# A state space layer inside a two-block transformer kernel, computed in chunks of four steps

## The reference

```python
bu = einsum('blgh,gph->blgp', u, bbar)            # drives, complex: re and im
x[t] = a * x[t-1] + bu[t]                         # scan over 256 steps, complex
y = einsum('blgp,ghp->blgh', xr, c_re) - einsum('blgp,ghp->blgh', xi, c_im) + d * u
y = gelu(y);  z = y @ w_glu + b_glu
out = z[:, :512] * sigmoid(z[:, 512:])
```

## Time and profile before

| | |
|---|---|
| profiled execution, its own time | 882.28 us |
| span, first to last instruction | 880.5 us |
| mean granted PE clock | 0.962 |
| busy: PE / PEld / DVE / ACT / POOL | 826.3 / 710.2 / 574.8 / 396.5 / 299.3 us |
| matmuls, vector, scalar, POOL instructions | 4933 / 856 / 614 / 248 |

### The profile page before, as it was taken

One profiled execution on the slowest core, in us unless ns is written; L12 is line 12 of the kernel. 1 busy time (PEld: TensorE's weight loads), 2 busy tenths in 40 slices (PEclk: granted clock), 3 DMA queues, 4 the chain that ended last, 5 costly groups with the idle time before them and its releaser, 6 DMA issues.

```text
span 880.5 us, 12434 instructions
## 1 busy us (share of the span) xinstructions
PE 826.3 (94%) x4933; PEld 710.2 (81%) x4933; DVE 574.8 (65%) x856; ACT 396.5 (45%) x614; POOL 299.3 (34%) x248
## 2 busy tenths in 40 slices
PE   7999999999999989999989998769896999999996
PEld 6889988998788889877778896435585999999884
DVE  4755957565674589656565569997657666666552
ACT  5644346334554433433774451212356544444441
POOL 3042801899010199998000024665401011111010
PEclk9999999999999999999999999787698999999998
DMA  7897893487305545645454642000244555665541
GB/s 205 194 249 240 193 243 85 121 187 173 96 26 194 164 127 191 211 121 164 144 192 144 190 156 84 1 0 1 71 144 143 161 176 177 182 192 192 192 167 48
DMA packets 77820, 130.79 MB, mean 149 GB/s; under 512 B 4286, under 2 KB 28210, under 8 KB 77634
## 3 DMA queue, kind: packets, MB, share of 16 engines
q1 hardware_dynamic: 76418, 125.10, 49.4%
q0 software_dynamic: 1200, 4.83, 1.7%
q10 hardware_dynamic: 144, 0.07, 0.0%
HBM read 128.91 MB, written 1.06 MB: 148 GB/s over the span
## 4 chain that ended last, share of the span: by engine, by line
PE 83%; DVE 11%; issue 2%; ACT 1%; DMA 1%; POOL 1%; DVEq 0%; SPq 0%; POOLq 0%; ACTq 0%
PE ps L1327 41%; PE ps L1344 16%; PE ps L1359 14%; PE ps L1446 2%; PE ps L1429 2%; PE ps L1580 2%; DVE ssm_b L1107 1%; DVE w_lo L762 1%; DVE ssm_a L1104 1%; PE ps L1273 1%; PE ps L1457 1%; PE ps L1458 1%; PE ps L1459 1%; DVE ssm_a L1099 1%; DVE ssm_b L1100 1%
## 5 line engine op out<-in xcount | busy, mean ns | idle before, releaser
L762 DVE TENSOR_TENSOR w_lo<-stage,w_hi 128x1024 fp32r<-128x1024 f32 x232 | 301.8, 1319 | 192.2 <-ACT w_hi L524 191.7
L524 ACT ACTIVATE w_hi<-stage 128x1024 fp32r<-128x1024 f32 x232 | 243.4, 1060 | 264.1 <-PE ps L1327 117.2
L1327 PE MATMUL ps<-w_hi,act_t 128*128 128x512 f32 (+1 forms) x768 | 253.5, 393 | 3.7 <-DVE act_t L799 2.1
L1327 PEld LDWEIGHTS ps<-w_hi,act_t 128*128 128x128 f32 x768 | 145.2, 190 | 38.0 <-issue 4.8
L1327 PE MATMUL ps<-w_lo,act_t 128*128 128x512 f32 (+1 forms) x448 | 174.8, 390 | 0.0
L1344 PE MATMUL ps<-act_t,w_hi 128*128 128x256 f32 x832 | 151.9, 284 | 2.5 <-DVE w_lo L762 2.5
L1344 PEld LDWEIGHTS ps<-act_t,w_hi 128*128 128x128 f32 x832 | 130.9, 193 | 3.0 <-DVE w_lo L762 2.7
L1359 PE MATMUL ps<-act_t,w_hi 128*128 128x256 f32 x704 | 127.4, 284 | 0.0
L1344 PE MATMUL ps<-act_t,w_lo 128*128 128x256 f32 x416 | 117.6, 283 | 0.0
L1359 PEld LDWEIGHTS ps<-act_t,w_hi 128*128 128x128 f32 x704 | 110.1, 192 | 0.0
L1359 PE MATMUL ps<-act_t,w_lo 128*128 128x256 f32 x352 | 99.7, 283 | 0.0
(11 more groups left out here) (309 smaller groups left out, 1201.7 us busy)
## 6 DMA issues: line engine op xcount, KB each, us to landing
stage<-in_even_w_in SPq DMA_DIRECT2D x64, 512.0 KB, 5.8
stage<-in_odd_w_in SPq DMA_DIRECT2D x48, 512.0 KB, 4.3
stage<-in_w_gate_up SPq DMA_DIRECT2D x44, 512.0 KB, 4.5
stage<-in_w_down SPq DMA_DIRECT2D x22, 512.0 KB, 3.9
stage<-in_even_w_out SPq DMA_DIRECT2D x16, 512.0 KB, 3.8
stage<-in_odd_w_out SPq DMA_DIRECT2D x16, 512.0 KB, 3.7
stage<-in_w_in SPq DMA_DIRECT2D x10, 512.0 KB, 3.6
stage<-in_w_out SPq DMA_DIRECT2D x8, 512.0 KB, 4.4
```

The lines of the kernel that those rows point to most:

```text
L524: nc.scalar.activation(w_hi[:, u % RING, :], stage[:, u % RING, :], ACT.Copy).then_inc(hi_ready, 1)
L762: nc.vector.tensor_tensor(w_lo[:, u % RING, :], stage[:, u % RING, :], w_hi[:, u % RING, :].bitcast(F32), ALU.subtract).then_inc(lo_ready, 1)
L1327: ins = mm(out[:, b, :], left, right, start=(k == 0 and n == 0), stop=(k == k_tiles - 1 and n == 2))
```

## The change

The 256 tokens are cut into 64 chunks of four steps. The state is scanned over the 64 chunk ends alone; what happens inside a chunk is matmul work with constants.

- **Constants.** POOL multiplies B and C by powers of the decay `a`: three for B, four for C (`times_a`, six operations of 128x512 each). PE turns four instead of one B (`turn_b`: 16 transposes after the second half of the queries, 16 after the keys of the dilated attention), and ACT copies them, eight copies of 128x512. After the retention keys PE makes the lag matrices (what an input does to the next three outputs within a chunk): 64 matmuls into 32 rows each, 32 or 96 columns wide; ACT copies them, POOL adds the skip term and makes the last power of C. The waves are only 64 long: two calls of `waves` instead of eight, one set of three ACT operations instead of four.
- **Drives.** `ssm_drives`: 128 matmuls of 32 input rows and 64 columns, between the queries' and the keys' projection; four in turn use the four strips of 32 rows and write to four banks. DVE then does four rounds (`ssm_drive`, `ssm_scan`) instead of 16, with the same tile sizes as one step before.
- **Outputs.** `ssm_lags`: 16 matmuls of 128 input rows and 256, 192, 128 or 64 columns, ahead of the attention. `ssm_states`: four times 32 matmuls into 32 rows, 63 columns wide, three between the heads and one behind them. They add up in PSUM, where ACT reads them for the gelu; the skip operation on DVE is gone.
- **Order.** ACT and DVE split the weights of the second half of `mix_attn` ahead of the turned result of the state space layer.
- **End.** The last three units of the last chunk are multiplied for the first 128 tokens, then for the second; the squares, the root and the output of the first block follow on their own.

All four rounds of drives and the rotation of the keys now stand ahead of the first head, and only the last scan behind it. The core of the diff, first POOL and ACT, then PE, DVE and the end of PE's program:

```diff
+            def times_a(dst, src, tmp, conj):
...
+                for own, other, op in ((0, 1, ALU.add if conj else ALU.subtract), (1, 0, ALU.subtract if conj else ALU.add)):
+                    TT(part(tmp[:, 0, :]), part(src[:, own, :]), ar, ALU.mult)
+                    then(TT(part(tmp[:, 1, :]), part(src[:, other, :]), ai, ALU.mult))
+                    ins = TT(dst[:, own, :], tmp[:, 0, :], tmp[:, 1, :], op)
...
+            then(nc.gpsimd.memset(lag[:], 0.0))
+            pool.wait_ge(b_wide_ready, 2)
+            for k in (1, 2):
+                times_a(b_pow[k], b_pow[k - 1], pow_tmp_early, False).then_inc(b_pow_ready, 1)
+                pool.wait_ge(b_pow_ready, k)
             scale_gates(0)
...
-            for i in range(3):
-                waves(i)
+            times_a(b_pow[3], b_pow[2], b_turn[:, 3, :, :, :].rearrange("p c t n -> p c (t n)"), False).then_inc(b_pow_ready, 1)
...
+            pool.wait_ge(b_turned, 2)
+            for k in (2, 3):
+                times_a(c_pow[k], c_pow[k - 1], c_pow[4], True).then_inc(c_pow_ready, 1)
...
+                    for part in range(2):
+                        ahead((("qb", "kb")[part], 1))
+                        act.wait_ge(b_turned, part + 1)
...
+                        for i in range(4):
+                            nc.scalar.activation(b_turn[:, 2 * part + i // 2, i % 2], bank(4 + i).rearrange("p (t n) -> p t n", t=CT), ACT.Copy).then_inc(b_ready, 1)
...
+            for part, kind in enumerate(("qb", "kb")):
+                for c in range(2):
+                    channels((kind, c))
+                turn_b(part)
+            pe.wait_ge(b_ready, 8)
             values_and_attention(1)
...
+            def ssm_drives():
+
+                chunk_drained(pe, ("u", 0))
+                for ct in range(CT):
+                    for c in range(2):
+                        for j in range(STEP):
+                            for q in range(4):
+                                r = slice(32 * q, 32 * q + 32)
+                                ins = mm(drive[:, ct, c, q, :], b_turn[r, STEP - 1 - j, c, ct, :], u_p[r, ct, j, :], start=(j == 0), stop=(j == STEP - 1))
+                ins.then_inc(drive_done, 1)
+
+            def ssm_lags():
+
+                pe.wait_ge(drive_read, CT)
+                pe.wait_ge(lag_ready, 1)
+                for ct in range(CT):
+                    for k in range(STEP):
+                        mm(y_of(ct)[:, k:STEP, :], lag[:, k, ct, :], u_p[:, ct, 0:STEP - k, :], start=(k == 0 and ct % 2 == 0), stop=False, skip_group_check=True)
+
+            def ssm_states(ct):
+
+                pe.wait_ge(state_ready, ct + 1)
+                for j in range(STEP):
+                    for c in range(2):
+                        for q in range(4):
+                            r = slice(32 * q, 32 * q + 32)
+                            ins = mm(y_of(ct, r)[:, j, 1:NC], c_pow[j + 1][:, c, ct * P + 32 * q:ct * P + 32 * q + 32], ssm_a[:, ct, c, q, 0:NC - 1],
+                                     start=False, stop=(c == 1), skip_group_check=True)
...
+            def ssm_between(i, part):
+                if part == 1 and i in (1, 3, 5):
+                    ssm_states(i // 2)
...
+            for ct in range(CT):
+                ssm_drive(ct)
+                if ct < 2:
+                    ssm_scan(ct)
+            chunk_drained(dve, ("skv", 0))
+            rope(SINK_H, KV_H)
+            ssm_scan(2)
...
+            for b in range(NB):
+                tok = slice(b * P, (b + 1) * P)
+                for j in range(KF // 2 - DOWN_LAST, KF // 2):
...
+                ins.then_inc(block_done, 1)
```

More of the change, by code:

```diff
@@ L48 @@
 UNIT = 1024
-SSM_BUFS = 4
-SSM_EARLY = 6
-SSM_STEPS = (2, 2) + 9 * (1,)
+STEP = 4
+NC = S // STEP
 AHEAD = 3
+DOWN_LAST = 3
 MASKS_AT, TABLES_AT = 20, 42
@@ L465, in _ @@
             root(1, D)
-            for i in range(3, 8):
-                waves(i)
+            pool.wait_ge(lag_copied, 4)
+            skip = mixed[:, 1, 0:512].rearrange("p (t n) -> p t n", t=CT)
+            for ct in range(CT):
+                ins = nc.gpsimd.tensor_scalar(skip[:, ct, :], ident[:], col[:, COL_SKIP + ct:COL_SKIP + ct + 1], None, ALU.mult)
+            then(ins)
+            nc.gpsimd.tensor_tensor(lag[:, 0], lag[:, 0], skip, ALU.add).then_inc(lag_ready, 1)
+            pool.wait_ge(lag_ready, 1)
+            then(times_a(c_pow[4], c_pow[3], b_pow[0], True))
+            then(nc.gpsimd.tensor_tensor(sp["fade"][:], sp["mag"][:], sp["mag"][:], ALU.mult))
+            then(nc.gpsimd.tensor_tensor(sp["fade"][:], sp["fade"][:], sp["fade"][:], ALU.mult))
+            nc.gpsimd.memset(fade[:, :, 0:1], 0.0)
+            nc.gpsimd.tensor_scalar(fade[:, :, 1:NC], sp["fade"][:].unsqueeze(2).to_broadcast([P, ST, NC - 1]), 1.0, None, ALU.mult).then_inc(fade_ready, 1)
             for h in range(RET_H):
@@ L472, in _ @@
                 nc.gpsimd.tensor_tensor(ret_rstd[:, h, :], ret_rstd[:, h, :], neg_half[:, 0:2], ALU.pow).then_inc(ret_scale, 1)
+            pool.wait_ge(late_in, 16 * 3)
+            pool.wait_ge(ret_decayed, RET_H)
+            for i in range(2):
+                waves(i)
             root(2, D)
@@ L656, in _ @@
             split_hi(chunks[("u", 0)][0] + 5)
+            act.wait_ge(wave_ready, 1)
+            then(nc.scalar.activation(cos_t, sin_t, ACT.Abs))
+            nc.scalar.activation(sin_t, sin_t, ACT.Sin)
+            nc.scalar.activation(cos_t, cos_t, ACT.Sin, bias=half_pi[:], scale=-1.0).then_inc(wave_sin, 1)
             act.wait_ge(h_ready, 2)
@@ L712, in _ @@
             nc.scalar.activation(gate_z[:], gate_z[:], ACT.Sigmoid).then_inc(sig_ready, 1)
-            ahead(("glu", 0))
+            ahead(("mix_attn", 1))
             hi_of_turned(3 * KD + 20, 4, 4, COL_GSSM)
@@ L746, in _ @@
             ahead(("down", 1))
-            chunk_done(act, ("down", 1))
-            squares_half_down(1, 0, result(("down", 1))[:, 0, :]).then_inc(squared, 1)
-            act.wait_ge(down_scaled_b, 1)
-            squares_half_down(1, 1, result(("down", 1))[:, 1, :]).then_inc(squared, 1)
+            for b in range(NB):
+                act.wait_ge(block_done, b + 1)
+                squares_half_down(1, b, result(("down", 1))[:, b, :]).then_inc(block_squared, 1)
         @block.vector
@@ L1479, in _, with turn_b @@
             pe.wait_ge(c_ready, 1)
-            pe.wait_ge(b_ready, 1)
             values_and_attention(0)
-            for name in (("qb", 0), ("qb", 1), ("kb", 0), ("kb", 1)):
-                channels(name)
+            def turn_b(part):
+                pe.wait_ge(heads_out, 2)
+                pe.wait_ge(b_wide_ready, 2)
+                pe.wait_ge(b_pow_ready, 2 * part + 1)
+                if part:
+                    pe.wait_ge(b_ready, 4)
+                for i in range(4):
+                    for ct in range(CT):
+                        ins = nc.tensor.transpose(bank(4 + i, P, ct * P), b_pow[2 * part + i // 2][:, i % 2, ct * P:(ct + 1) * P], ident[:])
+                ins.then_inc(b_turned, 1)
+            for part, kind in enumerate(("qb", "kb")):
[3 more added lines that the diff above has]
+            pe.wait_ge(b_ready, 8)
             values_and_attention(1)
@@ L1653, in _ @@
                 start_chunk(name)
-                for j in range(KF // 2):
+                for j in range(KF // 2 - c * DOWN_LAST):
                     tokens_unit(name, j, lambda k: ff_hi[:, k, :], lambda k: ff_lo[:, k, :], KF, lambda k: pe.wait_ge(ff_lo_ready, k // 2 + 1))
+            for b in range(NB):
+                tok = slice(b * P, (b + 1) * P)
+                for j in range(KF // 2 - DOWN_LAST, KF // 2):
+                    hi, lo = unit_of(name, j)
+                    for i in range(2):
+                        k = 2 * j + i
+                        passes = ((ff_hi[:, k, tok], hi[:, i, :]), (ff_hi[:, k, tok], lo[:, i, :]), (ff_lo[:, k, tok], hi[:, i, :]))
+                        for n, (left, right) in enumerate(passes):
+                            ins = mm(result(name)[:, b, :], left, right, start=False, stop=(k == KF - 1 and n == 2))
+                ins.then_inc(block_done, 1)
 _INPUTS = [
```

288 lines of the change are left out of this document (144 added, 144 removed).

## The result

The changed kernel takes 834.72 us (median of 4 runs, 831.95 to 841.16); the kernel before took 881.27 (878.98 to 882.96) beside it, with a fourth execution added to the three known before. The ratio is 0.9482, with a 95% interval of 0.9446 to 0.9517.

A forecast was written before the change was run, and what follows sets the result against it. DVE was taken to set the pace of the state space and window attention stage, PE that of the rest. 882.28 + 9.1 - 32.8 - 2.1 = 856.5 us, so 855 at the median; eight-in-ten range 841 to 874.

The forecast's parts named there:

- the heads' pace: Window attention: two heads depend on the two before, 8.1 us per period, two periods.
- Behind the turned result nothing changes in size: After the state space result is turned: no time change; the gelu reads PSUM in place of SBUF.
- Up to the drives: PE's path before the mixing stage: 9.1 us more, from B's transposes 3.1, a wait 2.3, lag matrices 3.7.
- Both at nothing: POOL's early powers and the later powers that replace the waves: no cost to PE.
- Drives: Start of the mixing stage: 32 groups of four row strips at 0.23 us each, 7.4 us.
- the end: Behind the last matmul: one square and two additions remain, 2.1 us less.
- The prediction's other price for the drives: From the Trainium skill: about threefold for four row strips, making the drives about a third longer than 7.4 us.
- The rival of column strips one after another: Lag matrices and state blocks on PE: strips run singly, 36.2 us more, 891 us; chance 0.06.
- The stage goes back to full clock and groups cost their columns: Mixing stage on PE: full clock, small-matmul groups priced by columns, 839 us; chance 0.16.
- Two at a time: Small matmuls on PE run only in twos, group terms of 19.2 us double, 874 us; chance 0.11.
- the fourth rival: Heads keep waiting on DVE operations slowed by POOL, or the early wait costs over 2.3 us: 866 to 880; chance 0.07.
- the early wait: PE's wait for `b_ready` 8, ahead of `values_and_attention(1)`, for ACT's last four copies of B: 2.3 us.

The follow-up runs named there:

- The kernel before with shorter waves: Kernel before, with the waves' angle reduction on POOL left out, nothing else moved: 876.35 against 882.58 us, ratio 0.9949.
- keys first: Changed kernel with DVE rotating the keys behind two of four rounds and lag products behind the second pair's scores: 832.11 us, ratio 0.9442.
- blocks behind: Changed kernel with the first three state blocks behind the next pair's scores instead of ahead of them: 833.08 us, ratio 0.9448.
- fillers: Changed kernel with 70 unused matmuls of 128 columns put into PE's wait for the keys: 841.78 us, ratio 0.9543.
- half drives: Changed kernel with drives of 32 instead of 64 columns, the same in number: 838.36 us in one execution.
- the serial run: Changed kernel with drives, lag matrices and state blocks doing one strip wholly before the next: 866.24 us, ratio 0.9829.
- a lighter load: Changed kernel with 36 unused products of 128 x 256 elements on POOL in retention: 837.14 us, ratio 0.9491.

## Why the prediction was wrong

**The step that failed** is the heads' pace, "At full clock 6.4 us, at half clock 3.3 more, 9.7; in the middle 8.1". A pair of heads took 5.07 us, twice (581.11 to 586.18 to 591.25), and the tail, from the seventh head's exponentials to the turned result, 7.7 in place of 9.9. Of the 3.0 us by which 8.1 was too long, 1.7 are the clock: it was granted in full from 582 to 598 us, where I had taken the mean of the two levels. 0.8 are the block, 1.0 in place of 1.8, as its groups of four cost 0.14 and not 0.23 us. 0.5 are the chain of maximum, exponentials and PE, 4.06 in the run with the blocks moved against 4.6 (6.4 less 1.8). In all this stretch gained 8.0 us more than forecast.

The clock's share belongs to this execution. In the second profile of the same kernel, the period from the third to the fifth head ran at half clock and took 7.28 us, and the eight heads 25.3; the next period was at full clock again, 5.08. The windows of that first period, in the first profile and then in the second:

```profile
581.11:586.18 5.07, 4.09 (x90) 3.36 (x89) 1.58 (x11) 3.56 (x11) 0.00 (x0) 0.97 0.00 0
```

```profile
582.54:589.82 7.28, 6.29 (x87) 5.21 (x86) 1.55 (x11) 3.56 (x11) 0.00 (x0) 0.52 0.00 0
```

Of the seven profiles with these heads in this order, four had the long period (7.2 to 7.3 us) and three the short one. At either level the sum was too long: 7.28 against 9.7 at half clock, 5.07 against 6.4 at full.

**The second is "Behind the turned result nothing changes in size".** 5.2 us went there. The windows show the larger part: the slow attention of the kernel before handed a PE at half clock to the mixing, 0.67 in its first 10.5 us, and the changed kernel 1.00. PE's wait of 0.56 us for `w_lo` went too. The 1.6 us from the transposes of x on lie in the product `down`: its 264 matmuls of 512 columns took 394 ns each before and 389 after, at a clock of 1.00 in both, and they start 0.2324 and 0.2267 us apart. Two of the groups, before and after:

```profile
L1327 PE MATMUL ps<-w_hi,ff_hi 128*128 128x512 f32 x88 | 34.7, 394 | 0.0
```

```profile
L1382 PE MATMUL ps<-w_hi,ff_hi 128*128 128x512 f32 x76 | 29.6, 389 | 0.0
```

The kernel before with shorter waves also has 394, and all eleven further runs of the changed kernel have the 389, so it comes with the program and not with the execution. Why is open.

**The third is a pair of errors that cancel.** Up to the drives +9.1 was forecast and +9.3 measured, but not of the same parts. The transposes were 2.6 (24 at 0.109), not 3.1; the wait 2.15, and 1.75 for the dip behind it that I did not count; the lag matrices 2.0 in place of 3.7: 8.5 in all. "Both at nothing", for POOL's powers, missed what the waves in whose place the later ones stand had cost (short waves: 4.5 us), which the changed kernel no longer pays at that place. And this execution paid some 6 us for half clock in the first heads, which others do not: in the four later kernels with the same order up to there and the full clock (keys first, blocks behind, fillers, half drives) the drives start at 534.6 to 536.4, only 1.0 to 2.8 us later than before. The median's gain, 5.4 us above the profile's, fits that.

**What was right.** Drives 7.37 (7.4 forecast); from them to the first exponentials 33.0 (35.0): no earlier than before, as said; lag products 6.9 (6.5); the third head 5.26 us behind the first (5); the end 2.3 (2.1). One gap on PE ahead of the keys' transposes was forecast, 9 us, and is there with 9.23. DVE's busy time fell by 57 us, more than the 45 given.

**The number for the drives was right for a wrong reason.** I took 0.23 us for one matmul and four in the time of one. Alone a matmul of one row strip takes two passes of 0.063, 0.125 us at full clock, and a group of four 0.23: four strips run 2.2 times as fast as one (0.063 / 0.028), not four. The prediction's other price for the drives, a third longer than 7.4, did not come either. For the column strips of a block it is 2.9 (3.14 / 1.09, both at a clock of 1.00), for the lag matrices 2.2 (4.5 / 2.0). The rival of column strips one after another is refuted by the serial run, and with it, for this kernel, the rule of the Trainium skill, "TensorE: Matmul & The Clock Gate", Part 3 ("What overlaps and what doesn't"), that a load overlaps only where the row group differs: a block's four strips share all rows.

The Trainium skill, "TensorE: Matmul & The Clock Gate", section "LDWEIGHTS (loading the stationary operand)", says that a weight load takes the time of its columns and not of its rows. The trace agrees: in the changed kernel a load of 32 rows and 128 columns lasted 0.187 us (the drives), one of 128 rows and 128 columns 0.188 (the end of `down`; 0.140 in the transposes of `y_attn`), and one of 128 rows and 32 columns 0.110 (the state blocks).

**The rivals.** "The stage goes back to full clock and groups cost their columns", at 839, came nearest, with 0.16, but not by its terms. It had the level of the clock in the heads of the first profile, with 6.4 us a period where 5.07 came; its lag products were wrong (6.9, at half clock for the most part), and the drives did not follow their columns. "Two at a time" and "one after another" did not occur. Of the fourth rival, the early wait did cost more than 2.3 us, 3.9 with the dip behind it, but other terms outweighed it.

## What to carry to other kernels

When the engine that sets a stage's pace is relieved, price the new chain at each level of TensorE's clock and give the two results their chances, rather than take the middle: here a period took 5.07 or 7.28 us, and which of the two differed between profiles of one program. Count also what the slow stage did to others, the clock that it hands on and the shared work of POOL and DVE, since both come back outside the lines that the diff touches. And look for order before instructions: moving blocks, keys and copies won another 11 us here.

## What the runs showed that was not expected

PE's records can be full while its clock falls: with one row strip at a time PE was busy for 8.00 of 8.00 us at a granted clock of 0.50, and with drives of 32 columns for 2.00 of 2.00 at 0.57. Grouped drives of 64 columns kept 1.00 throughout.

An idle POOL is worth something to DVE: the same splits took 1.78 us beside the waves and 1.29 beside shorter ones (means over the stage 1.57 and 1.28). The Trainium skill, "SBUF — State Buffer", "Who interferes with whom", puts such a loss down to a port pair that these two engines share, held by one at a time. The short waves agree in direction; a lighter load slowed the splits by 0.13 us only.
